# Attention rounds shifted: where the turned probabilities are copied, subtracted and used

## The reference

```python
def block(args):
    qi, fi, bi = args
    q_pos = bi * Q_BLOCK + jnp.arange(Q_BLOCK)
    logits = jnp.einsum('bhqd,bhkd->bhqk', qi, k) * scale + (fi[..., :, None] - cum_f[..., None, :])
    logits = jnp.where(k_pos[None, :] <= q_pos[:, None], logits, -jnp.inf)
    p = jax.nn.softmax(logits, axis=-1)
    return jnp.einsum('bhqk,bhkd->bhqd', p, v)
```

## Time and profile before

| | us |
|---|---|
| median of 3 runs | 4385.77 |
| lowest, highest | 4383.34, 4387.92 |
| profiled execution, its own time | 4383.03 |
| its span | 4381.4 |
| stage A, layers 1 and 2 | 107.0, 106.5 |
| stage CB, layers 1 and 2 | 122.0, 121.0 |
| forget stage | 322.0 |

### The profile page before, as it was taken

The page is one execution under the profiler, slowest core; times in us unless marked ns, Lnnn a source line. Parts: engine busy times, 40 slices in busy tenths (PEclk is TensorE's granted clock), DMA queues, the critical chain, the costliest instruction groups (busy, mean ns, idle before and its releaser), DMA issues.

```text
span 4381.4 us, 51384 instructions
## 1 busy us (share of the span) xinstructions
PE 4066.4 (93%) x17788; PEld 3216.0 (73%) x17788; DVE 1714.9 (39%) x2847; ACT 1505.5 (34%) x2448; POOL 369.0 (8%) x374
## 2 busy tenths in 40 slices
PE   8999978799999999967899989899999999789999
PEld 6887755588878887745688868787777668567888
DVE  3323565433323323664433234334432223534442
ACT  3222323432223223324332234435534553533331
POOL 1100011101001100011011000000100000100110
PEclk9999976799999999968799979999899999899999
DMA  3333310023323323200023324131112113222332
GB/s 102 96 97 97 82 42 20 1 82 96 96 82 91 96 96 93 76 19 20 29 82 96 96 86 112 39 83 44 39 54 72 39 44 91 58 73 76 96 98 98
DMA packets 495308, 316.51 MB, mean 72 GB/s; under 512 B 10832, under 2 KB 476368, under 8 KB 494640
## 3 DMA queue, kind: packets, MB, share of 16 engines
q1 hardware_dynamic: 490992, 302.86, 23.8%
q0 software_dynamic: 3008, 9.57, 0.7%
q10 hardware_dynamic: 1152, 2.10, 0.1%
HBM read 309.77 MB, written 4.33 MB: 72 GB/s over the span
## 4 chain that ended last, share of the span: by engine, by line
PE 68%; issue 21%; DVE 3%; ACT 3%; POOL 2%; PEld 1%; DVEq 1%; POOLq 0%; PEldq 0%; ACTq 0%
PE bank L214 19%; PE bank L216 19%; PE bank L215 19%; PE bank L256 1%; PE bank L1728 1%; PE bank L1734 1%; PE bank L1748 1%; PE bank L1737 1%; POOL h_lo L299 1%; PE bank L1028 1%; PE bank L1039 0%; PE bank L1030 0%; PE bank L1031 0%; PE bank L1149 0%; PE bank L648 0%
## 5 line engine op out<-in xcount | busy, mean ns | idle before, releaser
L214 PE MATMUL bank<-h_hi,w_hi 128*128 128x512 f32 (+3 forms) x3240 | 1297.9, 401 | 58.6 <-DVE w_lo L206 29.8
L215 PE MATMUL bank<-h_hi,w_lo 128*128 128x512 f32 (+3 forms) x3240 | 1279.0, 395 | 0.0
L216 PE MATMUL bank<-h_lo,w_hi 128*128 128x512 f32 (+3 forms) x3240 | 1277.7, 394 | 0.0
L206 DVE TENSOR_TENSOR w_lo<-w_raw,w_hi 128x1024 fp32r<-128x1024 f32 x571 | 737.7, 1292 | 1189.4 <-ACT w_hi L199 1183.4
L199 ACT ACTIVATE w_hi<-w_raw 128x1024 fp32r<-128x1024 f32 x571 | 598.4, 1049 | 596.4 <-DMA w_raw<-in_ffn_w_down 320.0
L214 PEld LDWEIGHTS bank<-h_hi,w_hi 128*128 128x128 f32 (+3 forms) x3240 | 612.1, 189 | 228.0 <-ACT lru_x L1831 31.0
L216 PEld LDWEIGHTS bank<-h_lo,w_hi 128*128 128x128 f32 (+3 forms) x3240 | 611.2, 189 | 140.5 <-issue 3.8
L215 PEld LDWEIGHTS bank<-h_hi,w_lo 128*128 128x128 f32 (+3 forms) x3240 | 612.5, 189 | 134.0 <-issue 4.6
L214 PE MATMUL bank<-g_hi,w_hi 128*128 (+1 forms) x880 | 342.3, 389 | 0.0
L215 PE MATMUL bank<-g_hi,w_lo 128*128 (+1 forms) x880 | 342.3, 389 | 0.0
L216 PE MATMUL bank<-g_lo,w_hi 128*128 (+1 forms) x880 | 342.3, 389 | 0.0
(11 more groups left out here) (382 smaller groups left out, 4404.1 us busy)
## 6 DMA issues: line engine op xcount, KB each, us to landing
w_raw<-in_w_in SPq DMA_DIRECT2D x161, 512.0 KB, 3.8
w_raw<-in_ffn_w_gate SPq DMA_DIRECT2D x88, 512.0 KB, 3.8
w_raw<-in_ffn_w_up SPq DMA_DIRECT2D x88, 512.0 KB, 3.8
w_raw<-in_ffn_w_down SPq DMA_DIRECT2D x88, 512.0 KB, 3.5
w_raw<-in_w_up SPq DMA_DIRECT2D x44, 512.0 KB, 3.7
w_raw<-in_w_branch SPq DMA_DIRECT2D x32, 512.0 KB, 3.8
w_raw<-in_w_out SPq DMA_DIRECT2D x24, 512.0 KB, 3.8
w_raw<-in_w_down SPq DMA_DIRECT2D x22, 512.0 KB, 3.5
```

The source lines that it names most:

```text
L206: dve.tensor_tensor(WL[:, slot(c), 0:w], RAW[:, slot(c), 0:w], WH[:, slot(c), 0:w].bitcast(F32), ALU.subtract).then_inc(w_lo, 1)
L214: pe.matmul(bank, wh, xh, start=start, stop=False)
L215: pe.matmul(bank, wl, xh, start=False, stop=False)
L216: return pe.matmul(bank, wh, xl, start=False, stop=stop)
```

## The change

Rounds are dealt out anew in all five stages (TT is 4):

- ACT copies turned step n-4 in round n (before: n-3), and before the pair's output and the splits of that round, which stood ahead of it.
- DVE subtracts turned step n-5 (before: n-3) and does so first in its round, ahead of the hook and the score pass; it stood last.
- PE makes the value product in rounds 9, 13, 17 ... (before: 7, 11, 15), after the scores of steps with i = 1 (before: i = 3).
- In the layers' stages a third turned bank is used (bank 6), so that a turning of step m needs the subtraction of step m-3; and with `late` the copies and subtractions of a head's first step are put off one round and stand together with those of its second. The forget stage keeps two banks and has no `late`.
- The forget stage has 70 rounds, over which the same 26 projection parts are spread.

No instruction is added or removed but a few that set registers.

```diff
@@ -967,8 +968,8 @@
             return self.parts[part][:, kt * KEY_STRIDE + kt * P:kt * KEY_STRIDE + S]

     def layer_places(parts):
-        return Places(lambda n, w: B[n % 2][:, 0:w], lambda m, a, b: B[2 + m % 2][:, a:b], 2,
-                      lambda m, w: (SG[:, 0, 0:w], SG[:, 1, 0:w], TMP[:, 0:w], T[:, 0, 0:w])[m % 4], parts)
+        return Places(lambda n, w: B[n % 2][:, 0:w], lambda m, a, b: B[(2, 3, 6)[m % 3]][:, a:b], 3,
+                      lambda m, w: (SG[:, 0, 0:w], SG[:, 1, 0:w], TMP[:, 0:w], T[:, 0, 0:w])[m % 4], parts, late=True)
...
@@ -999,8 +1000,14 @@
         for _ in attend_dve_parts(*args, **kw):
             pass

+    def turned_at(m, n, late):
+
+        if late and m % TT < 2:
+            return [] if m % TT == 0 else [k for k in (m - 1, m) if 0 <= k < n]
+        return [m] if 0 <= m < n else []
+
     def attend_pe_parts(pe, steps, n0, l0, h0, s0, y0, at, hook=None, banks=2):
-        for n in range(len(steps) + LAG + 1):
+        for n in range(len(steps) + TT + 2):
...
                 last.then_inc(qk_done, 1)
-            if n >= LAG + TT and (n - LAG) % TT == 0:
-                h = (n - LAG) // TT - 1
+            if n > 2 * TT and n % TT == 1:
+                h = n // TT - 2
...
@@ -1034,28 +1041,36 @@
             if LAG <= n < len(steps) + LAG:
                 m = n - LAG
                 pe.wait_ge(nrm_done, n0 + (m + 1))
-                pe.wait_ge(pl_done, l0 + (m + 1))
+                pe.wait_ge(pl_done, l0 + (m + 3 - at.n_turned))
...
-    def pair_taken(steps, n):
-
-        at = n - LAG - 8
...
     def attend_act_parts(act, steps, n0, h0, s0, y_of, jobs, waits, at):
...
-        for n in range(len(steps) + LAG + 1):
+        for n in range(len(steps) + TT + 2):
             if n < len(steps):
                 w = steps[n]["width"]
                 act.wait_ge(smax_done, n0 + (n + 3))
                 p = at.probs(n, w)
                 act.activation(p, p, ACT.Exp, bias=MX[:, n % 4:n % 4 + 1], scale=-1.0,
                                accum_out=SUM[:, n % 4:n % 4 + 1]).then_inc(exp_done, 1)
+            for m in turned_at(n - TT, len(steps), at.late):
+                w = steps[m]["width"]
+                act.wait_ge(tr_done, n0 + (m + 3))
+                if m % TT == 0:
+                    act.wait_ge(hv_done, h0 + (m // TT + 1))
+                act.activation(at.block(0, steps[m]), at.turned(m, 0, w).rearrange("p (k c) -> p k c", c=P), ACT.Copy
+                               ).then_inc(pt_done, 1)
+            if n >= 13 and n % 8 == 5:
+                pair = (n - 13) // 8
+                act.wait_ge(hv_done, h0 + (2 * pair + 3))
+                for bank, dst_hi, dst_lo in y_of(steps[8 * pair]["group"]):
+                    act.activation(dst_hi, B[bank][:, :], ACT.Copy).then_inc(y_hi, 1)
+            if n < len(steps):
                 pair = n // 8
...
@@ -1065,24 +1080,16 @@
...
-            if LAG <= n < len(steps) + LAG:
-                m = n - LAG
+            yield
+
+    def attend_dve_parts(dve, steps, n0, y0, y_of, at, hook=None):
+        dve.drain()
+        for n in range(len(steps) + TT + 3):
+            for m in turned_at(n - TT - 1, len(steps), at.late):
                 w = steps[m]["width"]
-                act.wait_ge(tr_done, n0 + (m + 3))
-                if m % TT == 0:
-                    act.wait_ge(hv_done, h0 + (m // TT + 1))
-                act.activation(at.block(0, steps[m]), at.turned(m, 0, w).rearrange("p (k c) -> p k c", c=P), ACT.Copy
-                               ).then_inc(pt_done, 1)
-            pair = pair_taken(steps, n)
-            if pair is not None:
-                act.wait_ge(hv_done, h0 + (2 * pair + 3))
-                for bank, dst_hi, dst_lo in y_of(steps[8 * pair]["group"]):
-                    act.activation(dst_hi, B[bank][:, :], ACT.Copy).then_inc(y_hi, 1)
...
-
-    def attend_dve_parts(dve, steps, n0, y0, y_of, at, hook=None):
-        dve.drain()
-        for n in range(len(steps) + LAG + 1):
+                dve.wait_ge(pt_done, n0 + (m + 3))
+                dve.tensor_tensor(at.block(1, steps[m]), at.turned(m, 0, w).rearrange("p (k c) -> p k c", c=P),
+                                  at.block(0, steps[m]).bitcast(F32), ALU.subtract).then_inc(pl_done, 1)
             if n < len(steps):
                 x = steps[n]
...
@@ -1102,14 +1109,8 @@
...
-            if LAG <= n < len(steps) + LAG:
-                m = n - LAG
-                w = steps[m]["width"]
-                dve.wait_ge(pt_done, n0 + (m + 3))
-                dve.tensor_tensor(at.block(1, steps[m]), at.turned(m, 0, w).rearrange("p (k c) -> p k c", c=P),
-                                  at.block(0, steps[m]).bitcast(F32), ALU.subtract).then_inc(pl_done, 1)
-            pair = pair_taken(steps, n)
-            if pair is not None:
+            if n >= 14 and n % 8 == 6:
+                pair = (n - 14) // 8
...
@@ -1605,7 +1606,7 @@

     SM, SF = LAYERS * N_STEPS, LAYERS * N_STEPS + 16
     YM, YF, YS = 16, 24, 32
-    MEM_STEPS_AND_TAIL, FOX_STEPS_AND_TAIL = 16 + LAG + 3, 64 + LAG + 1
+    MEM_STEPS_AND_TAIL, FOX_STEPS_AND_TAIL = 16 + LAG + 3, 64 + TT + 2
```

More of the change, by code:

```diff
@@ L954, in build, with __init__ @@
     class Places:
-        def __init__(self, scores, turned, n_turned, probs, parts=None):
+        def __init__(self, scores, turned, n_turned, probs, parts=None, late=False):
             self.scores, self.turned, self.n_turned, self.probs, self.parts = scores, turned, n_turned, probs, parts
+            self.late = late
         def block(self, part, x):
@@ L1042, in attend_pe_parts @@
             yield
-    def pair_taken(steps, n):
-        at = n - LAG - 8
-        return at // 8 if at >= 0 and at % 8 == 0 else None
     def attend_act_parts(act, steps, n0, h0, s0, y_of, jobs, waits, at):
```

1 line of the change is left out of this document (removed).

## The result

| | before | after |
|---|---|---|
| median, us | 4386.85 | 4458.46 |
| lowest to highest | 4383.34 to 4391.35 | 4455.11 to 4462.85 |
| span of the profiled execution | 4381.4 | 4461.2 |

The ratio is 1.0163, with a 95% interval of 1.0146 to 1.0181: slower by 72 us, where 38 had been forecast, within the range of 4386 to 4470. The clock line of the page shows where, against the earlier trace rows: in the layers' first dip (slices 6 to 8) it reads 7, 7, 8 where it read 7, 6, 7, and in the forget stage it is low in four slices (27 to 30) instead of one (29).

The account below looks back on a forecast made before the run. It took the engines' chain to bound the layers' stages and PE the forget stage; -22 us and +60 us gave +38, so 4424 us for the median, range 4386 to 4470, chance 0.60.

Parts of the forecast that it names:

- The forget stage's waits: Forget stage: PE's turnings wait for DVE's subtractions, 11.2 us in eight rounds for some 2 before; +60 us in all.
- Both causes: Forget stage: subtraction behind a projection's head norm, 2.6 or 2.1 us; ACT held at a copy by the value product, 5.2 us.
- +90 if each long wait also drops the clock: Forget stage: upper bound of its cost, if matmuls behind each long wait also run at a lower clock.
- Rival (c): Layers gain nothing; long waits drop the forget stage's clock, +60 to +90: 4446 to 4476 us; chance 0.20.
- The table load: ACT's load in the head norm: 1.28 us by the row; the skill's 2.66 would add some 17 us over the stage.
- The layers' stages: A and CB of both layers: shorter DVE waits, 5 us less per A and 6 per CB, together -22 us.
- the tail: Last heads of a layers' stage: lose 1.3 us, as the last-but-one head's value product stands between turnings.
- the layout by hand: CB, per head without splits: 9.0 to 8.5 us at full clock, 10.9 to 11.1 at half; with splits 11.1 to 9.7, 12.1 to 12.2.
- Rival (b): Layers' stages: denser PE gets full clock, -60 us against +60 in the forget stage: 4386 us; chance 0.11.
- Rival (a): Forget stage hides the waits and costs 2 us, so the layers' -22 decide: 4366 us; chance 0.09.
- signs named ahead: Forget stage: L1046 waits 60 us or more, L1035 none, 5 us behind every second value product, stage some 380 us.
- the gain of that move: Layers' stages: splits now behind the copy no longer delay it, about 1.2 us in one head of two.

Follow-up runs that it names:

- the early subtraction: Changed kernel, with DVE in the forget stage subtracting step n-4 at the end of round n: 4416.11 us, ratio 1.0056.
- the earlier value product: Changed kernel, forget stage with step n-4 subtracted at the end of round n and value product one round earlier: 4381.63 us, ratio 0.9993.
- the transposes: Kernel with the layers' change alone, plus four unused transposes ahead of each round's scores in CB: 4347.43 us, ratio 0.9912.
- the first run with idle matmuls: Changed kernel with 12 and 6 idle matmuls ahead of two turnings per eight rounds in the forget stage: 4451.19 us, ratio 1.0144.

## Why the prediction was right, and where its sizes were off

- **The forget stage's waits: right, in place and in sum.** Forecast for a turn were 5.2, 2.1 (2.6 without L630), 0.8, 0.3, 1.5 and 1.3 us, together 11.2; the trace has 4.95, 3.02, 0.84, 0.34, 0.35 and 1.74, together 11.24. Over the stage PE's idle time goes from 318.9 - 303.2 = 15.7 to 424.4 - 348.7 = 75.7 us: +60.0, the forecast's sum. The sum is closer than its terms, for two of them miss in opposite directions (3.02 us for 2.1, 0.35 for 1.5). Both causes that it named are shown, DVE's place behind the norm by the early subtraction, ACT standing at the copy by the earlier value product.
- **The term that was too small: the clock in the forget stage, "+90 if each long wait also drops the clock".** The prediction took the waits alone as the likeliest value and left the clock to the upper bound, and even that was short. The same 1360 matmuls take 45.5 us more. The row that should have decided it was there: by the earlier trace rows and the 1.4 us of the earlier trace rows the clock was at 0.89 with short waits alone, which is 71 us of the stage at half clock already (0.11 x 2 x 322); waits of 3 and 5 us could only add to that. Rival (c) had this mechanism with +60 to +90 and nothing from the layers; it was the mechanism in the one stage, and wrong in the other. Filling the longest waits gave 36 us of matmul time back, 27.7 of it net.
- **That the total lies in the range is in part luck.** The forget stage cost 105.5 us, above its bound of 90, and the layers gave 31.4 where 22 were forecast. With the forecast gain the total would have been 4468, two short of the range's end at 4470.
- **The table load: by the row.** In the trace ACT's load takes 1.28 us again and the root follows at 3033.28, two hundredths behind its end. The 2.66 us that the Trainium skill gives ("ScalarE: Activation LUTs", What ACT_TABLE_LOAD costs) for a switch with its drain does not show here; with it the wait would have been 6.3 us, not 4.95.
- **The layers' stages: right in direction, a third too small.** Forecast -5 for A and -6 for CB; measured -8.4 and -9.0, -7.5 and -6.5, together -31.4 against -22. DVE's waits came out as forecast in CB (30.6 us for "about 30") and a little above in A (16.5 for 14). In A the stage gained more than that wait gave (8.4 against 6.9 us), where the working had taken 2.8 us off for the tail and for PE at half clock; but against the layers of the run with the forget stage alone the gain is 6.1, so this is within what stages differ by. In CB the layout by hand gave too little: redone, it gives 2.7 and 8.3 us at the two clocks before the 1.3 of the tail are taken off (the text has "about 3" and "about 9"), and 3.9 with the tail at the 0.74 that was measured, for 7.5 and 6.5. What the working passed over is what the gain hangs on: without the putting off of the first step's copy the stages are 35 us longer (444.6 against 409.3), without the third bank another 44 (488.9). Both stand among the parts of the change, and the working gives neither a price: it was right to credit the layers with a gain, but by the one wait that it followed and not because it had weighed these two.
- **Rival (b), the clock in the layers: it did not come, and its price is open.** In the change the clock of CB rose a little (0.69 and 0.71 to 0.74 twice); in A it went from 0.52 and 0.62 to 0.57 twice, so not up as a whole. Driven up to 0.82 and 0.88 in CB, it gave no net gain, but the transposes used up what it gave back. The condition that the rival took for CB was misread: 2.93 us is the longest gap in the earlier trace rows, while over the stage PE waited up to 5.6 us before, and in the change still up to 5.1 (for `b_k_lo`). The Trainium skill's advice in "TensorE: Matmul & The Clock Gate" (Why this matters for your kernels) is to keep TensorE busy without long gaps. The forget stage agrees, with 36 us of matmul time regained by filling its waits; for CB no run here settles it.
- **Rival (a)**, the forget stage hiding it all, is out by the 75.7 us of idle time. Most signs named ahead came out: L1046 waits 73.6 us (60 or more), L1035 waits only once (1.8 us), 5 us stand behind every second value product. The stage is 424 us, not 380.
- **A wait that the forecast did not have:** with the layers' part PE waits for GpSimd's k parts in front of a pair's first scores, up to 5.3 us, since the splits behind the copies come later. In CB these are 13.9 us, where the kernel before had 4.4 for the same tile, at a value product; in A it had 6.9 already, for 7.3 now. The forecast had only the gain of that move (1.2 us in one head of two); it did not ask who waits for the splits.

## What to carry to other kernels

Shifting a consumer by a round is free only if its buffers and its place within the round give the same distance as before: count the turnings that need it, and ask what is queued ahead of it on its engine, above all where another program is woven in. Where PE is the bound, price a wait of PE twice, with its length and with the matmuls behind it at the lower clock (here 60 us of waits and 45 of clock). Where it is not, filler work that raises the clock can cost what it brings, as the transposes in CB did; put it only where PE would wait anyway. A shift that helps in one stage is best given to that stage alone: here 4349.6 us, and 4337.9 with the splits moved ahead, against 4385.8 before and 4458.5 for the whole.

## What the runs showed of the hardware

The clock fell behind a wait of 2.16 us: in the first run with idle matmuls PE was busy up to 3028.4, idle until 3030.6, and from 3033 to 3039 it had 0.50. Behind the waits of 0.35 and 1.74 us in the changed kernel (before 3070.79 and 3073.57) it stood at 0.50 from 3073.8 to 3076.8 as well.

Matmuls of 512 columns in a row start 0.23 us apart at 1.00 and 0.43 at 0.50, while the rows give a single one 0.39 and 0.63 us. They overlap, so that a sum of the durations overstates a row of them: 12 idle ones took 2.96 us (0.39 + 11 x 0.23), where 12 x 0.39 had been expected.

In the changed kernel ACT's table load took 1.28 us, and the activation behind it started 0.02 us after its end (3033.26 and 3033.28).
